# Modulation tiles beside the key and value projections, and query tiles woven into attention, in a two-layer model kernel

## The chip, the cores and the metric

The kernel runs on one core of a Trainium2 chip. The metric is the device time of one execution in microseconds (us), median over runs. The engines are TensorE (PE, with its weight loads PEld), VectorE (DVE), ScalarE (ACT), GpSimd (POOL) and SyncE (SP), which issues the weight loads. PE writes to eight PSUM banks of 512 floats per partition.

## What is computed

The reference runs a hybrid layer (windowed attention and an RWKV-7 scan side by side, then a SwiGLU), and behind it two more blocks. The change touches only the front of the first layer, in fp32, for 256 tokens x and 256 context tokens xc with 2048 features:

```python
mod = silu(c) @ ada_w + ada_b              # 2048 x 12288: shifts, scales and gates; also for c_ctx
sh1, sc1, g1, sh2, sc2, g2 = split(mod, 6)
z  = modulate(rmsnorm(x,  norm1_g), sh1,  sc1)  @ w_in
zc = modulate(rmsnorm(xc, norm1_g), sh1c, sc1c) @ w_in
# columns of w_in: q (16 heads of 64), k and v (4 heads), then for RWKV r, k, v, decay, a, gate
q, k = axial_rope(q), axial_rope(k)
attn = windowed_gqa(q, k, v, kc, vc, sink)   # 32 blocks of 128 queries, softmax over 512 keys
kk = k_r * k_k;  kk = kk * rsqrt(max(sum(kk * kk), 1e-12))   # per RWKV head
```

Of mod, the first third (sh1, sc1) is needed before z. The rest, "late modulation", is needed only after RWKV.

## The kernel before

Each weight matrix is cut into tiles of 512 rows by 256 columns, 512 KB each. `weight_stream` writes out by hand the one order in which all tiles come (`TILES`). SP issues their loads in that order into a ring of six buffers `raw` (NRAW = 6): the load of tile j waits until tile j - 6 has been used. The loop order on every engine is that of the generators in `schedule`, which has to take tiles in just the order of the stream; `run_all` weaves generators by numbers of steps for each.

An fp32 product is made of fp32r halves. ACT copies a tile to its high half `wh` (L1326), and the low half `wl = raw - wh` is made by DVE for tiles of even number (L1766) and by POOL for odd ones (L2298). `split_ahead` issues these splits when a tile is taken, for the stream's next AHEAD = 3 tiles; four pairs of halves exist. A `gemm` tile is then 24 matmuls (L872): of 512 columns where x and the context go together ("both": w_k, w_v, w_wa, w_ka), of 256 where only x does (w_q, w_r, w_gd). w_va has 48 of 256.

A modulation tile ("ada", L832) isn't split: PE multiplies it straight from `raw` in four row groups of 32 columns. After four tiles ACT copies the partial sums (`part`), PE adds the groups with a small matmul (`ada_sum`, L841), and DVE adds the bias.

The stages before: 64 early modulation tiles woven with 64 memory tiles; normalization of context and x into `halves`; w_k (4 outputs of 4 tiles each), w_v (the same), w_wa, w_ka, w_va; then the 16 w_q tiles, each followed by one of 16 late modulation tiles; then attention with r and the gate (16 w_r tiles, 4 w_gd), two of these tiles for each half step of attention, and behind them the 112 late modulation tiles left, woven with `keys`; then a fence and RWKV.

`attn` is a generator of 65 steps: first scores of blocks 0 and 1 (L901); then for every block n one step with the transposes of its probabilities (L915) and the scores of block n + 2, and one step with its product with the values (L926). ACT and DVE do the softmax between. `ev_q` ends a w_q output: ACT copies the raw values (`tm`), PE rotates them (L880), POOL and DVE finish.

`keys` is a generator of 17 steps: eight squares on ACT with sums over each head on PE (L940), one step for maximum, root and reciprocal, and eight steps in which ACT widens the scales (`sq`), PE transposes them (L948) and DVE multiplies to `kk`.

Of the kernel before, what the change touches and what calls it, by code (L numbers as in the profile page):

```python
# [165 lines left out]
class Program:  # L166
# [67 lines left out]
    def names(self):  # L234
# [28 lines left out]
        self.parts = [al[:, 3072 + 256 * i:3328 + 256 * i] for i in range(2)]  # L263
# [30 lines left out]
    def schedule(self):  # L294
# [12 lines left out]
        for n in range(4):  # L307
            rest(self.gemm("w_k", n, range(4), both, "v2", lambda j, n=n: self.ev_shift2(j, self.kT, 2 * n, 8 + 2 * n)))
        for n in range(4):
            rest(self.gemm("w_v", n, range(4), both, "v2", lambda j, n=n: self.ev_shift2(j, self.vT, 2 * n, 16 + 2 * n)))  # L310
        rest(self.gemm("w_wa", 0, range(4), both, "v2", lambda j: self.ev_shift2(j, self.wdad, 0, 24)))
        rest(self.gemm("w_ka", 0, range(4), both, "s2", self.ev_kA))
        token_major = [(a, 256 * tb, "A", 0, ("HA", "HB")[a], tb) for a in range(2) for tb in range(2)]
        rest(self.gemm("w_va", 0, range(4), token_major, "s2", self.ev_vA))
# [99 lines left out]

    def ada_tile(self, t):
        pass
# [41 lines left out]
    def queries(self):  # L458
        self.ada_active = True
        for n in range(4):  # L460
            yield from self.gemm("w_q", n, range(4), self.xonly, "s", lambda j, n=n: self.ev_q(j, n))
        self.ada_active = False
# [165 lines left out]
    def keys(self):  # L628
        yield from range(17)
# [164 lines left out]
class Tensor(Program):  # L794
# [28 lines left out]
    def ada_tile(self, t):  # L823
        raw = self.raw_of(t).rearrange("p (c n) -> p c n", c=4)
        b = 2 + t.nt % 2
        if t.kg == 0:
            self.bank(b, "mod_v", t.nt)
        self.wait_ge("silu_v", "sc16")
        self.wait_ge(f"raw{t.j % NRAW}", t.j)
        for g in range(4):  # L830
            k = 4 * t.kg + g
            m = self.e.matmul(self.G(b)[32 * g:32 * g + 32, 0:256], self.sc16[:, 32 * k:32 * k + 32], raw[:, g, :],  # L832
                              start=(t.kg == 0), stop=(t.kg == 3), skip_group_check=True)
        m.then_inc(self.sig("ada_mm", t.a), 1)
        self.last_a = t.a

    def ada_sum(self, nt):
        self.wait_ge("part_s", nt)
        part = self.part(nt)
        for fb in range(2):  # L840
            m = self.e.matmul(self.G(2 + nt % 2)[:, 256 + 2 * fb:258 + 2 * fb], part[:, 128 * fb:128 * fb + 128], self.cst("sel", 2),  # L841
                              start=True, stop=True, skip_group_check=True)
        m.then_inc(self.sig("ada_end", nt), 1)
# [32 lines left out]
    def rope_product(self, R, raw, rot):  # L876
        x = 2 + R % 2 if R < 10 else 3
        self.bank(4 + x, "rope_v", (R, "sin"))
        self.wait_ge(*raw)
        self.e.matmul(self.X(x)[:, 0:256], rot, self.tm[R % 4], start=True, stop=True).then_inc(self.sig("rope_mm", R), 1)  # L880
# [52 lines left out]
    def keys(self):  # L933
        squares = self.A("sq")
        self.bank(0, "kk_v", "max")
        o = self.G(0)[:, 0:64].rearrange("p (b c h) -> p b c h", b=4, c=8)
        for c in range(8):
            self.wait_ge("kk_s", ("sq", c))
            for b in range(4):
                m = self.e.matmul(o[:, b, c, :], squares[:, c, 128 * b:128 * b + 128], self.blk[:, ::64], start=True, stop=True)  # L940
            m.then_inc(self.sig("kk_mm", c), 1)
            yield
        yield
        for c in range(8):
# [375 lines left out]
class Scalar(Program):  # L1320
# [46 lines left out]
    def ada_part(self, nt):  # L1367
# [5 lines left out]
        if nt >= 16:  # L1373
            self.wait_fence(self.hb_free)
        self.wait_ge("ada_mm", self.last_a)
        self.act(self.part(nt), self.G(2 + nt % 2)[:, 0:256], ACT.Copy).then_inc(self.sig("part_s", nt), 1)
# [60 lines left out]
    def ev_gd(self, job):  # L1437
        self.wait_ge("mm", job.n)
        for fb in range(2):
# [59 lines left out]
    def keys(self):  # L1499
        self.wait_ge("mm", self.used["HA"])  # L1500
        for c in range(8):
            self.act(self.A("sq")[:, c, :], self.kT[:, c, :], ACT.Square, scale=self.cst("k_k", 8)[:, c:c + 1]).then_inc(self.sig("kk_s", ("sq", c)), 1)
# [5 lines left out]
        yield  # L1508
        for c in range(8):
# [250 lines left out]
class Vector(Program):  # L1760
# [80 lines left out]
    def ada_sum(self, nt):  # L1841
        dst = self.mod[:, 4 * nt:4 * nt + 4].rearrange("p (f t) -> p f t", t=2)
        src = self.G(2 + nt % 2)[:, 256:260].rearrange("p (f t) -> p f t", t=2)
# [33 lines left out]
    def rope_rest(self, R, dst, sin):  # L1877
        x = 2 + R % 2 if R < 10 else 3
# [3 lines left out]
        self.tt(raw, self.X(x)[:, 0:256], sin, MUL).then_inc(self.sig("rope_v", (R, "sin")), 1)  # L1882
# [78 lines left out]
    def keys(self):  # L1961
# [4 lines left out]
        self.ts1(inverse, self.G(0)[:, 0:64], 1e-12, None, MAX).then_inc(self.sig("kk_v", "max"), 1)  # L1966
        self.wait_ge("kk_s", "rt")
        self.e.reciprocal(inverse, inverse).then_inc(self.sig("kk_v", "rc"), 1)
        yield
        for c in range(8):  # L1970
# [443 lines left out]
def memory(nc, base):  # L2414

    m = {}
# [54 lines left out]
    at("inv", 24 * K, [4, 8, 2])  # L2471
# [132 lines left out]
```

## Time and profile before

| what | us |
|---|---|
| median of 3 runs | 4450.2 (4447.34 to 4452.76) |
| the profiled execution's own time | 4439.16 |
| its span | 4437.4 |
| PE busy | 4060.0 (91%) |
| DVE, ACT, POOL busy | 1525.7, 1580.5, 1355.4 |
| mean DMA rate | 151 GB/s |

Busy time of PE says that an instruction was in flight, not that PE was at its peak. The granted clock is a share of 2.4 GHz: 1.00 is the upper of TensorE's two levels and 0.50 the lower, and a window's value is the mean over it. "idle before" in square brackets is the time that an engine stood idle before an instruction, with what released it. All times are counted from the start of the span.

### The profile page before, as it was taken

How to read it: one execution, taken by the hardware profiler on the slowest of the kernel's cores; microseconds unless marked ns; L12 is line 12 of the kernel's file. 1: busy time of each engine (PE TensorE's matmuls, PEld its weight loads, DVE VectorE, ACT ScalarE, POOL GpSimd, SP SyncE). 2: the span in 40 equal slices, each digit the busy share in tenths (PEclk: the TensorE clock that was granted, in tenths of full speed). 3: DMA queues.
4: the chain of work that ended last, by engine and by line, in shares of the span. 5: the costliest groups of instructions: out<-in, count | busy, mean ns of one | idle time of the engine just before them, and what ended most of it. 6: DMA issues, size and time to landing. Idle time of an engine off the chain costs nothing.

```text
span 4437.4 us, 95544 instructions
## 1 busy us (share of the span) xinstructions
PE 4060.0 (91%) x42564; PEld 3794.0 (86%) x42564; DVE 1525.7 (34%) x2074; ACT 1580.5 (36%) x1986; POOL 1355.4 (31%) x632
## 2 busy tenths in 40 slices
PE   6979999979988889999997999897999999999978
PEld 5867887558887889999997899797899999999978
DVE  2133233446664543233334233325222222222232
ACT  3332233421223344343343343334333333333333
POOL 2322231000001334444442343443333333333333
PEclk8989998979998999999998999998999999999989
DMA  5862253830001445555553444353544444444433
GB/s 211 300 243 90 96 195 103 326 149 4 4 5 69 153 143 185 183 183 183 185 176 121 139 168 149 127 175 128 169 165 162 153 151 149 160 159 160 146 126 134
DMA packets 181879, 668.39 MB, mean 151 GB/s; under 512 B 20288, under 2 KB 20288, under 8 KB 180704
## 3 DMA queue, kind: packets, MB, share of 16 engines
q1 hardware_dynamic: 175248, 642.07, 42.3%
q10 hardware_dynamic: 4944, 16.03, 1.0%
q8 instruction: 337, 5.52, 0.5%
q0 software_dynamic: 1280, 4.20, 0.2%
q14 instruction: 70, 0.57, 0.0%
HBM read 653.82 MB, written 8.39 MB: 149 GB/s over the span
## 4 chain that ended last, share of the span: by engine, by line
PE 84%; DVE 6%; ACT 4%; issue 3%; DMA 1%; POOL 1%; ACTq 0%; POOLq 0%; DVEq 0%; SPq 0%
PE ps L872 65%; PE ps L832 2%; PE ps L1075 2%; PE ps L1099 2%; PE ps L1089 1%; PE ps L1011 1%; ACT wh L1326 1%; DVE wl L1766 1%; ACT halves L1326 1%; PE ps L1314 1%; PE ps L901 1%; DVE tm L1769 1%; PE ps L814 1%; PE ps L1298 1%; PE ps L926 1%
## 5 line engine op out<-in xcount | busy, mean ns | idle before, releaser
L872 PE MATMUL ps<-halves,wh 128*128 128x256 f32 (+1 forms) x13632 | 2620.4, 293 | 118.1 <-DVE halves L1769 34.0
L872 PEld LDWEIGHTS ps<-halves,wh 128*128 128x128 f32 x13632 | 2188.6, 195 | 178.6 <-issue 86.1
L872 PE MATMUL ps<-halves,wl 128*128 128x256 f32 (+1 forms) x6816 | 1983.4, 291 | 0.0
L2298 POOL TENSOR_TENSOR wl<-raw,wh 128x1024 fp32r<-128x1024 f32 x508 | 1237.1, 2436 | 1994.5 <-ACT wh L1326 1994.3
L1326 ACT ACTIVATE wh<-raw 128x1024 fp32r<-128x1024 f32 x1016 | 1072.9, 1058 | 1511.6 <-PE ps L872 1302.9
L1766 DVE TENSOR_TENSOR wl<-raw,wh 128x1024 fp32r<-128x1024 f32 x508 | 694.5, 1368 | 2062.9 <-ACT wh L1326 2062.8
L872 PEld LDWEIGHTS ps<-halves,wl 128*128 128x128 f32 x6816 | 1328.5, 195 | 12.8
L872 PE MATMUL ps<-wh,halves 128*128 128x256 f32 x2688 | 497.5, 285 | 0.0
L872 PEld LDWEIGHTS ps<-wh,halves 128*128 128x128 f32 x2688 | 423.3, 192 | 10.2 <-issue 7.8
L872 PE MATMUL ps<-wl,halves 128*128 128x256 f32 x1344 | 380.6, 283 | 0.0
L2298 POOL TENSOR_TENSOR halves<-mix,halves 128x1024 fp32r<-128x1024 f32 (+1 forms) x16 | 30.2, 1900 | 773.3 <-ACT halves L1326 773.3
L872 PEld LDWEIGHTS ps<-wl,halves 128*128 128x128 f32 x1344 | 258.3, 192 | 0.3
L1326 ACT ACTIVATE work<-ps 128x512 f32<-128x512 f32 x170 | 100.2, 592 | 226.5 <-PE ps L872 167.8
L832 PE MATMUL ps<-raw,sc 128*32 128x256 f32 x1536 | 126.7, 414 | 5.8 <-DMA raw<-in_ada 5.3
L1075 PE MATMUL ps<-X,BT 64*64 64x64 f32 x2560 | 95.9, 222 | 6.7 <-issue 6.0
L1075 PEld LDWEIGHTS ps<-X,BT 64*64 64x64 f32 x2560 | 87.3, 138 | 11.0 <-issue 9.2
L1306 PE MATMUL ps<-const,xw 128*128 128x128 f32 x144 | 24.1, 299 | 78.7 <-DVE xw L1772 78.7
L1099 PE MATMUL ps<-Xt,T 64*64 64x32 f32 x2560 | 93.2, 221 | 2.9 <-issue 2.6
L1326 ACT ACTIVATE hbl<-ps 128x256 f32<-128x256 f32 (+1 forms) x96 | 43.7, 455 | 133.9 <-PE ps L915 60.3
L1099 PEld LDWEIGHTS ps<-Xt,T 64*64 64x64 f32 x2560 | 86.6, 137 | 4.2 <-issue 3.3
L1306 PEld LDWEIGHTS ps<-const,xw 128*128 128x128 f32 x144 | 16.6, 150 | 85.0 <-DVE xw L1772 85.0
L832 PEld LDWEIGHTS ps<-raw,sc 128*32 128x32 f32 x1536 | 33.3, 111 | 56.9 <-issue 32.6
(241 smaller groups left out, 2669.8 us busy)
## 6 DMA issues: line engine op xcount, KB each, us to landing
raw<-in_ffn SPq DMA_DIRECT2D x264, 512.0 KB, 3.9
raw<-in_ada SPq DMA_DIRECT2D x192, 512.0 KB, 5.2
raw<-in_w_kv SPq DMA_DIRECT2D x192, 512.0 KB, 3.4
raw<-in_w_in_b SPq DMA_DIRECT2D x160, 512.0 KB, 3.8
raw<-in_w_in_a SPq DMA_DIRECT2D x128, 512.0 KB, 3.5
raw<-in_mem SPq DMA_DIRECT2D x64, 512.0 KB, 5.6
raw<-in_w_out_a SPq DMA_DIRECT2D x48, 512.0 KB, 4.0
raw<-in_w_out_b SPq DMA_DIRECT2D x48, 512.0 KB, 4.0
```

Source lines behind the costliest of these rows:

```text
L814: m = self.e.matmul(self.X(x)[:, 0:T], self.ones, self.work4[q][:, c, :], start=(q == 0 and c == 0), stop=(q == 3 and c == 3))
L832: m = self.e.matmul(self.G(b)[32 * g:32 * g + 32, 0:256], self.sc16[:, 32 * k:32 * k + 32], raw[:, g, :], start=(t.kg == 0), stop=(t.kg == ...
L872: p = self.e.matmul(o, x, y, start=bi not in begun, stop=final and kc == 3 and m == 2, skip_group_check=True)
L901: self.e.matmul(self.X(n % 2), self.qT[r, c, 128 * qb:128 * qb + 128], self.kA[r, c // 4, :], start=True, stop=True).then_inc(self.sig("at ...
L926: m = self.e.matmul(self.X(3)[HALF[half], 128 * qb:128 * qb + 128], self.vA[:, k, 64 * kv:64 * kv + 64], pt[:, k, :], start=(k == 0), stop ...
L1011: m = self.e.matmul(o[h, s, c, :], lhs(r, s, d, c), rhs(r, s, d, c), start=True, stop=True)
L1075: m = self.e.matmul(o[h, c, :], q["BT"][h, s, c, :], q["X"][h, s, c, :], start=True, stop=True)
L1089: m = self.e.matmul(o[h, c, :], q["Xt"][h, s, c, :], self.even(T1[h, s, c, :], lv), start=True, stop=True)
L1099: m = self.e.matmul(o[h, c, :], T1[h, s, c, :], self.odd(q["Xt"][h, s, c, :], lv), start=True, stop=True)
L1326: return self.e.activation(out, in_, func, **kw)
L1766: return self.e.tensor_tensor(out, a, b, op)
L2298: return self.e.tensor_tensor(out, a, b, op)
```

## The change

The stream and the weaving get another order:

- Behind each of the 32 w_k and w_v tiles come three late modulation tiles (96), behind each of the 12 tiles of w_wa, w_ka and w_va two (24), and behind each of the first four w_q tiles two (8). That is all 128.
- The 12 other w_q tiles are woven with attention's first 24 steps, one tile to two steps; then the 20 tiles of r and the gate with the rest, again one to two, and with one step of `key_norms` each.
- `keys` is cut into `key_norms` (9 steps) and `key_scales` (8 steps). The scales run alone, after attention.
- Late modulation uses PSUM banks 4 and 5 in place of 2 and 3; its partial sums, the squares and `inv` lie elsewhere. The squares have two buffers, so the square of c waits for the sum of c - 2.

```diff
-    for name, n in (("w_k", 4), ("w_v", 4), ("w_wa", 1), ("w_ka", 1), ("w_va", 1)):
-        add(name, range(n))
-    late = [("ada", nt, kg) for nt in range(16, 48) for kg in range(4)]
-    for i, q in enumerate([("w_q", nt, kg) for nt in range(4) for kg in range(4)]):
-        names += [q, late[i]]
+    late = iter([("ada", nt, kg) for nt in range(16, 48) for kg in range(4)])
+    for name, n, beside in (("w_k", 4, 3), ("w_v", 4, 3), ("w_wa", 1, 2), ("w_ka", 1, 2), ("w_va", 1, 2), ("w_q", 1, 2)):
+        for w in [(name, nt, kg) for nt in range(n) for kg in range(4)]:
+            names += [w, *itertools.islice(late, beside)]
+    add("w_q", range(1, 4))
     add("w_r", range(4))
     add("w_gd", range(1))
-    names += late[16:]
...
+        late_ada = self.ada_rest()
+        key_value = [self.gemm("w_k", n, range(4), both, "v2", lambda j, n=n: self.ev_shift2(j, self.kT, 2 * n, 8 + 2 * n)) for n in range(4)]
+        key_value += [self.gemm("w_v", n, range(4), both, "v2", lambda j, n=n: self.ev_shift2(j, self.vT, 2 * n, 16 + 2 * n)) for n in range(4)]
+        run_all((chain(*key_value), 1), (limited(late_ada, 96), 3))
...
+        run_all((chain(*narrow), 1), (limited(late_ada, 24), 2))
         self.hb_free = self.fence()
-        self.late_ada = self.ada_rest()
-        run_all((self.queries(), 1), (limited(self.late_ada, 16), 1))
-        run_all((self.attn(), 1), (chain(self.r_and_gd(), alternate(self.late_ada, self.keys())), 2))
+        run_all((self.queries(range(1)), 1), (late_ada, 2))
         self.ada_end()
+        attention = self.attn()
+        run_all((self.queries(range(1, 4)), 1), (limited(attention, 24), 2))
+        run_all((self.r_and_gd(), 1), (attention, 2), (self.key_norms(), 1))
+        rest(self.key_scales())
...
+    def ada_bank(self, nt):
+        return (2 if nt < 16 else 4) + nt % 2
...
+    def key_norms(self):
+        self.wait_fence(self.hb_free)
         for c in range(8):
-            self.act(self.A("sq")[:, c, :], self.kT[:, c, :], ACT.Square, scale=self.cst("k_k", 8)[:, c:c + 1]).then_inc(self.sig("kk_s", ("sq", c)), 1)
+            if c >= 2:
+                self.wait_ge("kk_mm", c - 2)
+            self.act(self.A("sq2")[:, c % 2, :], self.kT[:, c, :], ACT.Square, scale=self.cst("k_k", 8)[:, c:c + 1]).then_inc(self.sig("kk_s", ("sq", c)), 1)
             yield
```

In the changed kernel L844 is the modulation matmul, L853 its sum, L884 the tile's matmuls, L913, L927 and L938 the scores, transposes and values of attention, L952 the key norms, L963 the key scales, and L1341 every operation of ACT.

The order of ACT where the normalization of context and x (`halves`) ends, before:

```order
 L1326 ACTIVATE wh<-raw 128x1024 x5
 L1326 ACTIVATE tm<-ps 128x256
 L1326 ACTIVATE work<-ps 128x512
 L1326 ACTIVATE halves<-tm,mod 128x256 x32
 L1326 ACTIVATE wh<-raw 128x1024 x4
 L1326 ACTIVATE xk<-ps,tsr 128x512 x2
```

and after the change:

```order
 L1341 ACTIVATE halves<-tm,mod 128x256 x32
 L1341 ACTIVATE wh<-raw 128x1024 x2
 L1341 ACTIVATE work<-ps 128x256
 L1341 ACTIVATE wh<-raw 128x1024
 L1341 ACTIVATE work<-ps 128x256
 L1341 ACTIVATE wh<-raw 128x1024
 L1341 ACTIVATE xk<-ps,tsr 128x512 x2
```

Before, three splits of w_k stand in front of the normalization and the fourth behind it; now one stands in front, since two of the next three tiles of the stream are modulation tiles. Copies of partial sums (`work<-ps`) stand between the splits.

The order of PE in the w_k stage after the change, between two tiles of w_k:

```order
L884 MATMUL ps<-halves,wl 128x512
L844 MATMUL ps<-raw,sc_109 32x256 x12
L853 MATMUL ps<-const,work 128x2 x2
L884 MATMUL ps<-halves,wh 128x512 x2
```

Three modulation tiles (twelve matmuls) and a sum have moved in there; before, the L872 rows of two tiles follow each other.

The order of PE at two key norms before:

```order
L832 MATMUL ps<-raw,sc_108 32x256 x4
L940 MATMUL ps<-const,sq 128x2 x4
L915 MATMUL ps<-const,hbl_71 128x128 x4
L901 MATMUL ps<-work,hb_q 128x512
L832 MATMUL ps<-raw,sc_108 32x256 x4
L940 MATMUL ps<-const,sq 128x2 x4
L926 MATMUL ps<-hbl_71,work 64x128 x4
```

and at one of them after, with the end of one w_r tile and the start of the next:

```order
L884 MATMUL ps<-halves,wl 128x256
L938 MATMUL ps<-hbl_71,work 64x128 x4
L927 MATMUL ps<-const,hbl_71 128x128 x4
L913 MATMUL ps<-work,hb_q 128x512
L952 MATMUL ps<-const,sq_105 128x2 x4
L884 MATMUL ps<-halves,wh 128x256 x2
```

The norm now follows the scores with nothing between, and a whole w_r tile stands between it and the next block's values.

## Rows read from the trace of the kernel before

**Rows 1.** The page's head

```profile
span 4437.4 us, 95544 instructions
```

**Rows 2.** Windows: length, busy us (instructions) of PE, PEld, DVE, ACT, POOL, clock, DMA share, GB/s

```profile
645.00:720.00 75.00, 75.00 (x562) 67.22 (x566) 36.97 (x69) 32.66 (x60) 22.92 (x12) 1.00 0.43 141
720.00:780.00 60.00, 51.69 (x264) 33.16 (x262) 15.07 (x44) 21.38 (x47) 0.00 (x0) 0.63 0.30 97
780.00:895.00 115.00, 110.81 (x1028) 61.27 (x1026) 47.36 (x148) 50.01 (x133) 0.00 (x0) 1.00 0.89 336
895.00:928.00 33.00, 26.20 (x231) 11.12 (x224) 1.14 (x7) 3.60 (x9) 0.00 (x0) 0.73 0.87 345
928.00:980.00 52.00, 38.47 (x833) 33.86 (x834) 29.07 (x41) 17.05 (x20) 0.00 (x0) 0.64 0.11 39
```

**Rows 3.** Timeline of PE (start, us, instruction, idle before) at the restart

```profile
353.68 1.19 PE L872 MATMUL ps<-halves,wh 128*128 128x512 f32 x2 [5.99 <-ACT wh L1326]
```

**Rows 4.** Evictions of w_k and w_v (min/median/max ns, first to last start); start of w_q

```profile
L1326 ACT ACTIVATE xk<-ps,tsr x8: 679/685/691, 361.2 to 427.1; 128x512 f32<-128x512 f32 x8
...
L1326 ACT ACTIVATE vT<-ps,tsr x8: 681/686/692, 448.3 to 514.2; 128x512 f32<-128x512 f32 x8
...
582.76 0.51 PE L872 MATMUL ps<-halves,wh 128*128 128x256 f32 x2 [0.69 <-ACT work L1326]
```

**Rows 5.** Timeline of the query stage; then DMA issues of 820 to 880 us

```profile
604.89 0.64 PE L832 MATMUL ps<-raw,sc 128*32 128x256 f32 x8
605.46 0.61 PE L841 MATMUL ps<-const,hbl 128*128 128x2 f32 x4
605.92 0.48 PE L872 MATMUL ps<-halves,wh 128*128 128x256 f32 x2
606.01 0.38 SPq L2393 DMA_DIRECT2D raw<-in_w_q  x1
610.74 1.06 ACT L1326 ACTIVATE wh<-raw 128x1024 fp32r<-128x1024 f32 x1 [2.87 <-DMA raw<-in_w_q]
611.95 2.37 POOL L2298 TENSOR_TENSOR wl<-raw,wh 128x1024 fp32r<-128x1024 f32 x1 [6.08 <-ACT wh L1326]
...
raw<-in_ada SPq DMA_DIRECT2D x45, 512.0 KB, 5.7
```

**Rows 6.** Timeline of one block of attention with a key norm

```profile
747.33 0.63 PE L915 MATMUL ps<-const,hbl 128*128 128x128 f32 x4
748.94 0.64 PE L832 MATMUL ps<-raw,sc 128*32 128x256 f32 x8
750.22 0.71 ACT L1326 ACTIVATE sq<-xk,const 128x512 f32<-128x512 f32 x1
750.99 1.05 PE L940 MATMUL ps<-const,sq 128*128 128x2 f32 x8 [0.87 <-ACT sq L1326]
751.16 0.49 DVE L1772 TENSOR_SCALAR hbl<-hbl,cols 128x512 f32<-128x512 f32 x1
751.97 1.09 PE L926 MATMUL ps<-hbl,work 128*64 128x128 f32 x8
752.99 0.67 PE L832 MATMUL ps<-raw,sc 128*32 128x256 f32 x8
```

**Rows 7.** Timeline: last rope, first scores, first scaling; the last modulation sum

```profile
644.98 1.10 PE L880 MATMUL ps<-tm,const 128*128 128x256 f32 x4
...
646.01 1.98 PE L901 MATMUL ps<-work,hb_q 64*128 64x512 f32 x4
...
651.81 0.49 DVE L1772 TENSOR_SCALAR hbl<-hbl,cols 128x512 f32<-128x512 f32 x1
...
926.57 1.01 PE L841 MATMUL ps<-const,hbl 128*128 128x2 f32 x4 [0.56 <-ACT hbl L1326]
```

**Rows 8.** Timeline: a low half of POOL and the scaling of probabilities on DVE

```profile
700.73 1.57 POOL L2298 TENSOR_TENSOR wl<-raw,wh 128x640 fp32r<-128x640 f32 x1 [6.17 <-ACT wh L1326]
700.79 1.79 DVE L1772 TENSOR_SCALAR hbl<-hbl,cols 128x512 f32<-128x512 f32 x1
```

More of the change, by code:

```diff
@@ L262, in names @@
         self.ptbuf = [al[:, 1536 + 512 * i:2048 + 512 * i].rearrange("p (b n) -> p b n", b=4) for i in range(3)]
-        self.parts = [al[:, 3072 + 256 * i:3328 + 256 * i] for i in range(2)]
+        self.parts = [wk[:, 7168 + 256 * i:7424 + 256 * i] for i in range(2)]
         self.sink = self.cst("sink", 16)
@@ L306, in schedule @@
         xonly = self.xonly
[L307 to L312, printed above, removed]
+        late_ada = self.ada_rest()
+        key_value = [self.gemm("w_k", n, range(4), both, "v2", lambda j, n=n: self.ev_shift2(j, self.kT, 2 * n, 8 + 2 * n)) for n in range(4)]
+        key_value += [self.gemm("w_v", n, range(4), both, "v2", lambda j, n=n: self.ev_shift2(j, self.vT, 2 * n, 16 + 2 * n)) for n in range(4)]
+        run_all((chain(*key_value), 1), (limited(late_ada, 96), 3))
         token_major = [(a, 256 * tb, "A", 0, ("HA", "HB")[a], tb) for a in range(2) for tb in range(2)]
-        rest(self.gemm("w_va", 0, range(4), token_major, "s2", self.ev_vA))
+        narrow = [self.gemm("w_wa", 0, range(4), both, "v2", lambda j: self.ev_shift2(j, self.wdad, 0, 24)),
+                  self.gemm("w_ka", 0, range(4), both, "s2", self.ev_kA),
+                  self.gemm("w_va", 0, range(4), token_major, "s2", self.ev_vA)]
+        run_all((chain(*narrow), 1), (limited(late_ada, 24), 2))
         self.hb_free = self.fence()
-        self.late_ada = self.ada_rest()
-        run_all((self.queries(), 1), (limited(self.late_ada, 16), 1))
-        run_all((self.attn(), 1), (chain(self.r_and_gd(), alternate(self.late_ada, self.keys())), 2))
+        run_all((self.queries(range(1)), 1), (late_ada, 2))
         self.ada_end()
+        attention = self.attn()
+        run_all((self.queries(range(1, 4)), 1), (limited(attention, 24), 2))
+        run_all((self.r_and_gd(), 1), (attention, 2), (self.key_norms(), 1))
+        rest(self.key_scales())
         self.rwkv()
@@ L456, in memory_kv, with queries @@
         self.ada_active = False
-    def queries(self):
+    def queries(self, ns):
         self.ada_active = True
-        for n in range(4):
+        for n in ns:
             yield from self.gemm("w_q", n, range(4), self.xonly, "s", lambda j, n=n: self.ev_q(j, n))
@@ L626, with key_scales @@
     bonus_begin = bonus_a = bonus_k = bonus_v = nothing
-    def keys(self):
-        yield from range(17)
+    def key_norms(self):
+        yield from range(9)
+    def key_scales(self):
+        yield from range(8)
     def out_mean(self, p):
@@ L876, in rope_product @@
     def rope_product(self, R, raw, rot):
-        x = 2 + R % 2 if R < 10 else 3
-        self.bank(4 + x, "rope_v", (R, "sin"))
+        b = self.rope_bank(R)
+        self.bank(b, "rope_v", (R, "sin"))
         self.wait_ge(*raw)
-        self.e.matmul(self.X(x)[:, 0:256], rot, self.tm[R % 4], start=True, stop=True).then_inc(self.sig("rope_mm", R), 1)
+        self.e.matmul(self.G(b)[:, 0:256], rot, self.tm[R % 4], start=True, stop=True).then_inc(self.sig("rope_mm", R), 1)
     def ev_kA(self, job):
@@ L929, in attn, with key_norms @@
             yield
[L933 to L936, printed above, removed]
+    def key_norms(self):
+        squares = self.A("sq2")
+        self.bank(2, "kk_v", "max")
+        o = self.G(2)[:, 0:64].rearrange("p (b c h) -> p b c h", b=4, c=8)
         for c in range(8):
@@ L939, in keys @@
             for b in range(4):
-                m = self.e.matmul(o[:, b, c, :], squares[:, c, 128 * b:128 * b + 128], self.blk[:, ::64], start=True, stop=True)
+                m = self.e.matmul(o[:, b, c, :], squares[:, c % 2, 128 * b:128 * b + 128], self.blk[:, ::64], start=True, stop=True)
             m.then_inc(self.sig("kk_mm", c), 1)
@@ L943, in keys, with key_scales @@
         yield
+    def key_scales(self):
+        squares = self.A("sq")
         for c in range(8):
@@ L1508, in keys, with key_scales @@
         yield
+    def key_scales(self):
+        inverse = self.A("inv")
+        self.wait_ge("mm", self.used["HA"])
         for c in range(8):
@@ L1881, in rope_rest @@
         self.wait_ge("rope_g", R)
-        self.tt(raw, self.X(x)[:, 0:256], sin, MUL).then_inc(self.sig("rope_v", (R, "sin")), 1)
+        self.tt(raw, self.G(self.rope_bank(R))[:, 0:256], sin, MUL).then_inc(self.sig("rope_v", (R, "sin")), 1)
         self.wait_ge("rope_v", (R, "sin"))
```

26 lines of the change are left out of this document (14 added, 12 removed).

## The prediction

> **What bounds the kernel now.** I read the table of windows first, because the change touches one stretch only. After the restart at 353.68 the sequence is: w_k and w_v tiles to about 513.5, the three narrow projections to 582.76, the queries to 646, r and the gate woven with the first heads to about 720, then heads with late modulation and key norms, then modulation tiles alone to 927.6, then RWKV. In the windows [rows 2] 645 to 720 is TensorE (PE) without a gap at granted clock 1.00. 720 to 780 has 51.7 us of work in 60 and clock 0.63, so most of it ran at the lower of the two levels (1.2 instead of 2.4 GHz). 895 to 928 has 26.2 in 33, clock 0.73, with the DMA share at 0.87: tiles that wait for their loads. So the stretch loses time in two ways: the slow clock beside thin work, and a transfer-bound tail. From 582.76 to 927.6 it takes 344.8 us. The same matmuls back to back at full clock would take about 300 (priced below). **About 45 us are to be had there, and that is the ceiling of any gain.** The view of order and the timeline rows say what the new order loses in their place.
>
> **Prices at full clock.** A "both" tile (w_k, w_v): evictions of xk go from 361.2 to 427.1 over 12 tiles, less the 0.6 between two evictions of a pair, 65.3 / 12 = 5.44 us; vT gives the same (65.9 - 0.6) / 12 [rows 4]. A modulation tile: 604.89 to 605.46, 0.57 us, and per four tiles one sum of 0.46 (605.46 to 605.92) [rows 5]: 0.685 each. An x-only tile: the query stage of 16 tiles lasts from 582.76 [rows 4] to 646.0 (behind the rope of 644.98, 1.10 us [rows 7]); less 16 modulation tiles (11.0) and four rope pairs (4.4) it is 47.8 / 16 = 3.0. One head-block of attention: transposes and next scores 747.33 to 748.94 = 1.61, values 751.97 to 752.99 = 1.02, together 2.63; one key norm 750.99 to 751.97 = 0.98 [rows 6]. Sum for 36 x-only tiles (108), 128 modulation tiles (88), 32 head-blocks (84), 8 norms and 8 scales at about 1.0 (16) and rope (4.4): 300.
>
> **The change, walked forward from the restart.**
>
> *Restart.* Before, three w_k tiles were split ahead of the normalization and multiplied during it; PE then waited 5.99 us for the fourth, whose split stands behind the normalization on ScalarE (ACT) [rows 3]. The planner splits three tiles of the stream ahead, and now these are one w_k tile and two modulation tiles, of which nothing is split. So at 353.68 only one w_k tile and three modulation tiles are done: two tiles lost, 10.9, less three modulation tiles, 2.1: **8.8 us**. The same PE start otherwise.
>
> *Key and value tiles.* Tile 1 ends at about 361.2, where tile 3 ended. 30 more at 5.44 + 3 x 0.685 = 7.49 are 224.7, and three last modulation tiles 2.1: 588.0. Transfers: 45 tiles in the 60 us from 820 to 880 are 1.33 us each [rows 5], so a group of four needs 5.3 of 7.5 us; bandwidth hides it. Latency nearly doesn't. The raw ring has six places, and a w tile's load is issued when the second modulation tile two groups ahead is done: E + 1.2, with E the end of the w tile before last. A w_q load as second of a pair is issued at 606.01 and split from 610.74 on, 4.7 later [rows 5]; the split takes 1.06, the low half on GpSimd 2.37 from 611.95 (on VectorE, every other tile, about half of it). Ready at E + 1.2 + 4.7 + 1.2 + 2.4 = E + 9.5; PE comes at E + 2.05 + 5.44 + 2.05 = E + 9.5. Every other tile is on the edge: I take 0.3 us for 15 of them, **4 us** (bounds 0 and, with the 5.7 us of the full queue, 15 x 1.3 = 20). 592.
>
> *Narrow projections.* Before 513.5 to 582.8, 69.3; 24 modulation tiles add 16.3: 677.6. Their groups are longer per load, nothing waits.
>
> *First query tile and the end of modulation.* 4 x 3.0 + 8 x 0.685 + rope 1.1 and 1.5 of waits at the two ends: 697.7. Transfers 12 x 1.33 = 16 are covered.
>
> *Heads, queries, r, gate.* 32 tiles x 3.0 = 96, 32 head-blocks x 2.63 = 84: 877.7 without waits. Each round is: tile, values of block n, transposes and scores. Scores end at 748.94, the probabilities of the next block are done at 751.65 (751.16 + 0.49) [rows 6]: 2.7 us, while PE has 3.0 + 1.0 of other work. Rounds without extras therefore lose nothing. Four places do:
> - Start: the second query tile covers nothing for the first transposes, since both first scores and the transposes stand behind it in one piece. Before, the softmax of block 0 took from the scores' start at 646.01 to the end of the scaling at 652.30 (651.81 + 0.49), 6.3, of which the scores are 2.0 [rows 7]; two r tiles covered the rest, now nothing does. The rope that delayed VectorE there comes a tile earlier, so I take **3.9 us** of the 4.3.
> - Rope of three query tiles: ACT's copies stand behind the exponent and the sink of that round, which is where the square starts, 750.22, 1.3 after the scores' end [rows 6]; with the copy itself the rotation waits about 1.75, and PE has nothing between: 3 x (1.1 + 1.75) = **8.6**, of which 3.3 is work.
> - Key norms: the order shows L952 right behind the scores. Its square on ACT comes behind the exponent too: from the scores' end at 748.94 to the norm's start at 750.99 are 2.05 [rows 6]; before, a modulation tile filled 1.1 of it and 0.87 was idle, now nothing fills it. 8 x (2.05 + 0.98) = **24.2**, and 1.5, an estimate, for ACT's table changes around the root.
> - Scales at the end: they stand alone. ACT first does the gate's copies, two tanh and a mix copy: PE idle 3.9, then 8 x 1.0 and 0.8 for the last product: **13**.
> 877.7 + 3.9 + 8.6 + 25.7 + 13 = 928.9.
>
> *The clock.* It was 1.00 where dense tiles ran without waits (645 to 720), 0.63 where heads, norms and waits of 0.9 to 2.7 us alternated [rows 2]. A key round now is 3.0 of dense work in 8.7. Bounds: no loss, or all eight rounds at half, 8 x 6.6 = 53. I take the end near the dense rows, 1.2 us a round, 10 in all, 2 at the start of attention and 3 in the scales: **15 us**.
>
> Sum: 943.9 where before has 927.6 (926.57 + 1.01 [rows 7]), **+16 us**. RWKV and what follows have the same order and the same fence, 0. The execution traced has a span of 4437.4 [rows 1] and a time of 4439.2: 4455. The median of the runs shown, 4450.2, is 11 above it, so 4466.
>
> **The rivals.** A measurement of this kernel tells apart about 0.2%, 9 us.
> 1. *The forecast*, +6 to +30: chance 0.42.
> 2. *Dense tiles hold the clock.* Every key round holds a full x-only tile; if that is enough, 15 us go and the stretch ends at 928.9, +1: no change. For it: clock 1.00 in 780 to 895, where no dense tile ran at all, though PE there was busy for 110.8 of 115 us [rows 2]. Against: PE idle 2.05 in each key round. 0.20.
> 3. *The other side: RWKV opens at full clock.* Before, PE entered it from a slow tail, and 928 to 980 has clock 0.64 on 38.5 us of work [rows 2]; 0.72 of these at half cost up to 14. If the clock holds in the key rounds too and PE enters with it, the end is +1 - 14 = -13, 4437. It decides from the point where less than 5 us of the clock loss is paid. Against: the wait for RWKV's own tables after the fence stays. 0.20.
> 4. *Loads set the pace beside w_k and w_v.* If the second load of a burst of four takes the 5.7 us of the full queue [rows 5] and not 4.7, GpSimd's tiles come 1.0 to 1.3 late each: 16 to 20 in place of 4, +30, 4480. 0.11.
> 5. *VectorE waits for GpSimd beside the heads.* The scaling of the probabilities took 1.79 us instead of 0.49 when GpSimd's low half started 0.06 ahead of it [rows 8]. All heads now run beside splits. With a low half of 2.37 starting first the probabilities would come 2.6 later, 1.2 after PE needs them, on the 16 rounds where GpSimd splits: 19 more, +35, 4485. Against: its split follows ACT's, which stands behind the exponent, so the scaling is usually first by 0.3. 0.07.
> The Trainium skill, "SBUF — State Buffer", section "Who interferes with whom", says why this could be: VectorE in a two-port mode and GpSimd lock one pair of ports for a whole instruction, and issue order decides who blocks. By that rule the price is paid in full whenever GpSimd is first, and the trace agrees (1.79 against 0.49); taken alone, without the 0.3 us of lead, it would give rival 5.
>
> **How the numbers follow.** The range 4436 to 4490 holds rivals 1, 2 and most of 3, 4 and 5. For the forecast alone it is 4456 to 4480. Slower by over 0.2%: 0.38 of the forecast and rivals 4 and 5, 0.56. Within: rival 2 and the rest of the forecast, 0.24. Faster: rival 3, 0.20.
>
> **What would show it.** PE's restart with tile 1 at 353.7 and the end of w_v near 592; PE idle at L952 about 2 us eight times; first rope of attention behind an idle of 1.8; the scales ending near 944; windows of the key rounds with clock 0.75 to 0.95. Wrong if low halves come late beside w_k by over 1 us each, if the key rounds show clock 1.00, or if RWKV's first 50 us differ in clock from before.

## The result, and the profile after

| | us | executions |
|---|---|---|
| before | 4449.43 | 4 (4447.34 to 4452.76) |
| after | 4481.92 | 4 (4473.66 to 4486.98) |

The ratio is 1.0071, interval 1.0053 to 1.0088: **0.7% slower, 32 us**. The profiled execution took 4481.41. Before's profiled one took 4439.16, 10 under its median, so the two traces lie 42 apart and not 32. The first 32 of them are in the stretch that the change touches: RWKV's first product starts at 936.40 before and 968.93 after.

The page's head, against [rows 1]:

```profile
span 4479.6 us, 95520 instructions
```

The restart on PE's timeline, which answers to [rows 3], and the last eviction of w_v on ACT's, which answers to [rows 4]:

```profile
353.27 1.19 PE L884 MATMUL ps<-halves,wh 128*128 128x512 f32 x2 [16.06 <-issue]
...
598.43 1.26 ACT L1341 ACTIVATE vT<-ps,tsr 128x512 f32<-128x512 f32 x2 [2.10 <-PE ps L884]
```

This is w_k's tile 1, as forecast: TensorE has stood for 16.06 us where before it stood for 5.99. With three modulation tiles behind it, w_v ends at 600.5 (598.43 and 2.1). What PE waited for from 353 to 600 (us in total, times, longest):

```profile
PE ps L884 <- issue: 16.4, 2, 16.1
PE ps L884 <- POOL wl L2319: 9.5, 13, 1.5
```

Thirteen times it was the low half that GpSimd makes of every other tile. From the first query tile to attention (PE's timeline, against [rows 5, 7]):

```profile
700.84 0.77 PE L884 MATMUL ps<-halves,wh 128*128 128x256 f32 x2 [1.70 <-POOL wl L2319]
...
707.52 0.48 PE L884 MATMUL ps<-halves,wh 128*128 128x256 f32 x2
...
710.55 1.12 PE L913 MATMUL ps<-work,hb_q 64*128 64x512 f32 x2
712.28 1.12 PE L913 MATMUL ps<-work,hb_q 64*128 64x512 f32 x2 [0.60 <-DVE mod L1786]
717.10 1.11 PE L927 MATMUL ps<-const,hbl 128*128 128x128 f32 x4 [3.70 <-DVE hbl L1792]
...
740.84 1.57 PE L892 MATMUL ps<-tm,const 128*128 128x256 f32 x4 [1.63 <-ACT tm L1341]
```

Modulation ends at 707.5; one query tile later come the first scores, and then 3.70 us of idle for the first probabilities. The first rope product inside attention waits 1.63. One round with a key norm, PE and ACT together, against [rows 6]:

```profile
844.85 0.71 ACT L1341 ACTIVATE sq<-xk,const 128x512 f32<-128x512 f32 x1
...
845.62 1.05 PE L952 MATMUL ps<-const,sq 128*128 128x2 f32 x8 [1.97 <-ACT sq L1341]
845.79 0.49 DVE L1792 TENSOR_SCALAR hbl<-hbl,cols 128x512 f32<-128x512 f32 x1
...
851.08 1.09 PE L938 MATMUL ps<-hbl,work 128*64 128x128 f32 x8
852.10 0.66 PE L927 MATMUL ps<-const,hbl 128*128 128x128 f32 x4
852.68 1.12 PE L913 MATMUL ps<-work,hb_q 64*128 64x512 f32 x2
...
855.77 1.05 PE L952 MATMUL ps<-const,sq 128*128 128x2 f32 x8 [1.97 <-ACT sq L1341]
```

From norm to norm it is 10.15 us (855.77 - 845.62). Work at the upper clock is 3.0 + 2.63 + 0.98 = 6.6 of it, 1.97 is idle for the square, and the rest, near 1.5, is lost because part of the tile behind runs at the lower clock. The end of the stretch:

```profile
945.56 1.09 PE L938 MATMUL ps<-hbl,work 128*64 128x128 f32 x8 [0.69 <-ACT hbl L1341]
949.56 9.65 PE L963 MATMUL ps<-const,sq 128*128 128x128 f32 x64 [2.91 <-ACT sq L1341]
968.93 1.97 PE L1001 MATMUL ps<-wup,lora 64*64 64x512 f32 x4 [9.72 <-DMA w0r<-in_w]
```

The windows, against [rows 2]:

```profile
353.00:600.00 247.00, 236.82 (x1576) 170.06 (x1580) 43.35 (x68) 50.75 (x69) 35.59 (x16) 0.99 0.73 258
600.00:710.00 110.00, 107.78 (x813) 86.47 (x805) 22.87 (x32) 26.65 (x38) 26.04 (x14) 0.98 0.69 244
710.00:800.00 90.00, 80.72 (x469) 62.87 (x468) 48.83 (x101) 39.21 (x86) 21.02 (x13) 0.89 0.28 89
800.00:880.00 80.00, 64.16 (x364) 53.78 (x364) 24.92 (x60) 29.60 (x62) 9.27 (x4) 0.84 0.17 50
880.00:944.00 64.00, 64.00 (x432) 51.27 (x431) 30.61 (x77) 31.99 (x72) 8.01 (x5) 0.99 0.06 17
944.00:970.00 26.00, 12.68 (x83) 10.90 (x83) 8.80 (x21) 9.08 (x18) 0.00 (x0) 0.80 0.21 74
```

The transfer-bound tail is gone, as the change meant. In its place 800 to 880 has 16 us without work and clock 0.84; 880 to 944, rounds of a tile and a head-block without a norm, has no idle time and clock 0.99. So the woven rounds as such are sound, and the norm is the first suspect for what spoils the others.

### The profile page after: what moved, and what is told of

It reads as the page before. It is cut to its first block, busy times and chain, and to the rows that moved or that the text cites. A ratio compares the mean times of both kernels' runs of the same rounds, so it can differ in the third digit from the quotient of the medians.

```text
span 4479.6 us, 95520 instructions
## 1 busy us (share of the span) xinstructions
PE 4071.7 (91%) x42564; PEld 3813.7 (85%) x42564; DVE 1533.6 (34%) x2074; ACT 1574.5 (35%) x1986; POOL 1349.9 (30%) x632
## 4 chain that ended last, share of the span: by engine, by line
PE 82%; DVE 6%; ACT 5%; issue 3%; DMA 2%; POOL 1%; ACTq 0%; POOLq 0%; DVEq 0%; SPq 0%
PE ps L884 63%; PE ps L1090 2%; PE ps L844 2%; PE ps L1114 2%; ACT wh L1341 2%; PE ps L1026 1%; PE ps L1104 1%; DVE wl L1786 1%; ACT halves L1341 1%; POOL wl L2319 1%; DMA raw<-in_w_v 1%; PE ps L826 1%; PE ps L1329 1%; DVE tm L1789 1%; PE ps L913 1%
## 5 line engine op out<-in xcount | busy, mean ns | idle before, releaser
L884 PE MATMUL ps<-halves,wh 128*128 128x256 f32 (+1 forms) x13632 | 2647.4, 295 | 137.1 <-DVE halves L1789 33.7
L884 PEld LDWEIGHTS ps<-halves,wh 128*128 128x128 f32 x13632 | 2204.0, 197 | 214.0 <-issue 131.2
L884 PE MATMUL ps<-halves,wl 128*128 128x256 f32 (+1 forms) x6816 | 1993.9, 293 | 0.0
L1341 ACT ACTIVATE wh<-raw 128x1024 fp32r<-128x1024 f32 x1016 | 1070.0, 1055 | 1543.7 <-PE ps L884 1176.7
L884 PEld LDWEIGHTS ps<-halves,wl 128*128 128x128 f32 x6816 | 1339.0, 196 | 13.6
L884 PE MATMUL ps<-wh,halves 128*128 128x256 f32 x2688 | 498.6, 285 | 0.1
L884 PEld LDWEIGHTS ps<-wh,halves 128*128 128x128 f32 x2688 | 423.9, 192 | 10.6 <-issue 9.2
L884 PE MATMUL ps<-wl,halves 128*128 128x256 f32 x1344 | 380.9, 283 | 0.0
L884 PEld LDWEIGHTS ps<-wl,halves 128*128 128x128 f32 x1344 | 258.5, 192 | 0.2
L1341 ACT ACTIVATE work<-ps 128x512 f32<-128x512 f32 (+1 forms) x202 | 112.3, 558 | 278.1 <-PE ps L884 169.0
L844 PE MATMUL ps<-raw,sc 128*32 128x256 f32 x1536 | 109.2, 387 | 0.0
L1090 PEld LDWEIGHTS ps<-X,BT 64*64 64x64 f32 x2560 | 88.6, 140 | 12.3 <-issue 11.1
L1104 PE MATMUL ps<-T,Xt 64*64 64x32 f32 x2048 | 77.1, 223 | 5.3 <-issue 5.3
L1104 PEld LDWEIGHTS ps<-T,Xt 64*64 64x64 f32 x2048 | 72.7, 141 | 10.4 <-issue 9.3
```

Of the source, the lines that this page charges most:

```text
L884: p = self.e.matmul(o, x, y, start=bi not in begun, stop=final and kc == 3 and m == 2, skip_group_check=True)
L1090: m = self.e.matmul(o[h, c, :], q["BT"][h, s, c, :], q["X"][h, s, c, :], start=True, stop=True)
L1104: m = self.e.matmul(o[h, c, :], q["Xt"][h, s, c, :], self.even(T1[h, s, c, :], lv), start=True, stop=True)
L1341: return self.e.activation(out, in_, func, **kw)
```

## The experiments

Each is compared with executions of the kernel before that ran beside it; the changed kernel stands at 1.0071. "RWKV" is the start of RWKV's first product in the trace.

| run | ratio to before (interval) | against the changed kernel, us | RWKV, us | against 968.93 |
|---|---|---|---|---|
| norms_first | 1.0004 (0.9992 to 1.0017) | -30 | 938.90 | -30.0 |
| norm_filler | 1.0043 (1.0026 to 1.0060) | -12 | 954.84 | -14.1 |
| filler_half | 1.0072 (1.0047 to 1.0097) | 0 | 965.92 | -3.0 |
| lows_vector | 1.0041 (1.0029 to 1.0054) | -13 | 957.12 | -11.8 |
| restart3 | 1.0035 (1.0024 to 1.0047) | -16 | 958.25 | -10.7 |
| rope_late | 1.0040 (1.0027 to 1.0054) | -14 | 956.63 | -12.3 |
| part1_only | 1.0080 (1.0063 to 1.0098) | +4 | 976.42 | +7.5 |
| combo | 0.9944 (0.9926 to 0.9962) | -57 | 912.51 | -56.4 |
| combo_unwoven | 1.0014 (0.9998 to 1.0029) | -25 | 940.64 | -28.3 |
| combo_start | 0.9937 (0.9915 to 0.9959) | -60 | 904.30 | -64.6 |

The third column is the difference of the ratios times 4450; since each interval is 5 to 11 us to either side, and the changed kernel's own is 8, a few us in it mean nothing. The last column is read from single traces, and agrees with it within 5.3 us in each run.

**norms_first: the key norm ahead of the attention steps.**

```
-        run_all((self.r_and_gd(), 1), (attention, 2), (self.key_norms(), 1))
+        run_all((self.r_and_gd(), 1), (self.key_norms(), 1), (attention, 2))
```

> In the rounds of r and the gate the key norm stands ahead of the two attention steps (right behind the r tile), on every engine; nothing else differs from the changed kernel. Theory: the 1.97 to 2.06 us in which TensorE waits eight times for ScalarE's square are a matter of order alone, since the square then runs while the r tile is multiplied; and the stretch of 3.4 us at the lower clock in each of these rounds is caused by that wait. Both go: 8 x 1.97 = 16 and 8 x 1.7 = 14, together 26 to 30 us less than the changed kernel, and the windows of these rounds show clock 1.00. Rival A: the wait moves, since the first transposes of the round now stand behind only a tile and a norm while the square has pushed ScalarE's exponent back: 8 x 0.5 to 1.5 us of waits at the transposes, gain 5 to 15. Rival B: the clock does not follow the wait, gain 13 to 16.

PE's timeline of one round, norm to norm, and its window:

```profile
805.38 1.05 PE L952 MATMUL ps<-const,sq 128*128 128x2 f32 x8
806.37 1.09 PE L938 MATMUL ps<-hbl,work 128*64 128x128 f32 x8
807.39 0.66 PE L927 MATMUL ps<-const,hbl 128*128 128x128 f32 x4
...
812.02 1.05 PE L952 MATMUL ps<-const,sq 128*128 128x2 f32 x8
...
800.00:860.00 60.00, 59.43 (x411) 48.27 (x409) 28.07 (x69) 34.95 (x71) 9.61 (x4) 1.00 0.21 67
```

The round is 6.64 us instead of 10.15, there are no brackets (no idle time), and the clock is 1.00. One line's order was worth 30 us, almost the whole loss of the change: the theory at its upper end. Rival A's waits at the transposes are not there. How much of the 30 was idle time and how much the slow clock behind it is told by the next two.

**norm_filler and filler_half: the wait filled with work that nobody reads.**

```
+        hi = self.acts["HA"][0]
+        self.wait_ge("rope_v", (9, "sin"))
         for c in range(8):
+            for k in range(14):
+                self.e.matmul(self.G(3)[:, 0:256], hi[:, k, 0:128], hi[:, k, :], start=True, stop=True, skip_group_check=True)
             self.wait_ge("kk_s", ("sq", c))
```

In filler_half the 14 is a 7.

> The changed kernel with 14 more products of 128x128 by 128x256 on TensorE ahead of each wait for a square (their result is read by nobody); they are sized at 14 x 0.125 = 1.75 us, to fill the wait of 1.97 and end inside it. Theory: the lower clock in the key rounds comes from TensorE's idle time there; with it filled the windows of these rounds show clock near 1.00 and the kernel is 8 x 1.4 to 1.7 = 11 to 14 us shorter than the changed one, although it does more work. Rival: the clock falls for another reason (the thin work of attention itself); then it is the same or up to 8 x 1.5 = 12 us longer, as the added products take twice their time at the lower clock.

> As the run with added products, but 7 instead of 14: they take about 0.96 us of the 1.97 us wait, so TensorE still idles about 1.0 us in each of the eight key rounds. Theory (the lower clock follows an idle time of some size): either the remaining 1.0 us is short enough, then the round is 8.65 us as with 14 products and the kernel is as fast as that one (12 us under the changed kernel); or it is not, then the round stays near 10.15 and nothing is won. Both tell how large an idle time beside dense tiles costs here; I give 0.7 to the first, as idle times of 0.5 to 0.7 us stand in stretches of clock 1.00.

With 14 products, and then with 7 (PE's timeline and a window of each):

```profile
801.77 1.93 PE L953 MATMUL ps<-halves 128*128 128x256 f32 x14
803.81 1.05 PE L956 MATMUL ps<-const,sq 128*128 128x2 f32 x8
...
812.46 1.05 PE L956 MATMUL ps<-const,sq 128*128 128x2 f32 x8
...
800.00:860.00 60.00, 59.24 (x417) 49.26 (x416) 21.05 (x50) 25.48 (x53) 7.20 (x3) 1.00 0.19 59
```

```profile
813.04 1.05 PE L956 MATMUL ps<-const,sq 128*128 128x2 f32 x8 [0.95 <-ACT sq L1345]
...
821.14 1.09 PE L953 MATMUL ps<-halves 128*128 128x256 f32 x7
823.18 1.05 PE L956 MATMUL ps<-const,sq 128*128 128x2 f32 x8 [0.95 <-ACT sq L1345]
...
820.00:840.00 20.00, 18.11 (x106) 15.30 (x105) 7.15 (x17) 7.67 (x17) 2.38 (x1) 0.83 0.16 45
```

TensorE does more work and the kernel is 12 us shorter: the round is 8.65 us, which is 1.5 less than 10.15, eight times. That is the clock's own share, and the idle time's is the rest, 8.65 - 6.64 = 2.0 a round. With half the filler 0.95 us of idle remains before each of the eight norms. The first round was still clean (804.39 to 813.04, 8.65 us); from the second on the clock is 0.83, the round 10.14 (823.18 - 813.04), and in the median nothing is won. I had given 0.7 to the other outcome. An idle time of a microsecond in each such round cost the clock as much as one of two.

**lows_vector: low halves of w_k and w_v on VectorE.**

```
+def low_on_gpsimd(t):
+    return t.n % 2 and t.name not in ("w_k", "w_v")
...
-        self.wait_ge("lo_g" if t.n % 2 else "lo_v", t.n)
+        self.wait_ge("lo_g" if low_on_gpsimd(t) else "lo_v", t.n)
```

> The changed kernel with the low halves of all 32 w_k and w_v tiles on VectorE, in place of every other one on GpSimd. Theory: the 11.2 us in which TensorE waits 14 times for GpSimd's low half are the ring's latency plus GpSimd's 2.37 us for a low half; VectorE does it in about half, so these waits go: 9 to 11 us less than the changed kernel, and w_v's last eviction about 590 in place of 599. Rival: the load lands late by itself and the waits move to the high half or stay; gain below 3 us.

The waits of 353 to 600, and the last eviction of w_v:

```profile
PE ps L888 <- ACT wh L1345: 14.9, 1, 14.9
PE ps L888 <- DVE wl L1790: 0.9, 3, 0.4
...
587.31 1.27 ACT L1345 ACTIVATE vT<-ps,tsr 128x512 f32<-128x512 f32 x2 [1.10 <-PE ps L888]
```

587.31 instead of 598.43, and 9.5 us of waits became 0.9, so the rival is refuted. The gain, 13 us by the ratios and 11.8 in the trace, is slightly more than the theory's 9 to 11. In the changed kernel the loads of w_k and w_v landed 4.5 us after their issue in the median (400 to 590 us), as in the forecast; the time of GpSimd's low half was what came on top.

**restart3: three w_k tiles ahead of the first modulation tile.** The modulation tiles displaced stand three to a narrow tile.

```
-            names += [w, *itertools.islice(late, beside)]
+            names += [w, *itertools.islice(late, beside if name != "w_k" or w[1:] > (0, 1) else 0)]
...
+        rest(limited(key_value, 2))
-        run_all((chain(*key_value), 1), (limited(late_ada, 96), 3))
+        run_all((key_value, 1), (limited(late_ada, 90), 3))
```

> The changed kernel with the first three w_k tiles next to each other in the stream again, so that three are split ahead of the normalization; the modulation tiles taken from there stand beside the narrow projections (three to a tile in place of two). Theory: the two tiles lost at the restart (10.9 us, less three modulation tiles, 2.1) come back: 8 to 9 us less than the changed kernel, and a wait of up to 6 us behind the third tile as in the kernel before, of which three modulation tiles cover 2. Rival: loads beside the narrow projections now come too densely (three small tiles and one large in 7.5 us) and give part of it back: gain 3 to 6.

```profile
354.11 1.19 PE L886 MATMUL ps<-halves,wh 128*128 128x512 f32 x2 [4.86 <-issue]
```

The wait at the restart (PE's timeline) is 4.86 in place of 16.06, with three w_k tiles done by then and not one, and attention's first scores come at 701.49 in place of 710.55, 9.1 earlier: the theory's 8 to 9. RWKV's start is 10.7 earlier and the measured ratio gives 16; the expectation holds for the trace, and the 5 us between it and the median lie within the intervals.

**rope_late: the rope product of TensorE behind the next weight tile.** Tensor's `ev_q` only notes the two products, and `products` issues them behind its last matmul.

```
+        self.late_rope = [(self.ropes + fb, ("ev_s", (job.key, fb - 1))) for fb in range(2)]
...
         p.then_inc(self.sig("mm", t.n), 1)
+        self.ropes_now()
```

> The changed kernel with TensorE's rope products of the last three query tiles issued behind the next weight tile, in place of ahead of it. Theory: the three waits of 1.63 to 1.72 us for ScalarE's copies and the stretch of 3.4 us at the lower clock behind each come from that position alone: 3 x (1.67 + 1.7) = 10 us less than the changed kernel. Rival: the clock stays down here, because the first of these stretches stands close to the start of attention: gain 5.

```profile
739.11 1.03 PE L893 MATMUL ps<-tm,const 128*128 128x256 f32 x4
740.07 1.09 PE L947 MATMUL ps<-hbl,work 128*64 128x128 f32 x8
...
735.00:760.00 25.00, 25.00 (x161) 18.99 (x160) 14.22 (x30) 12.79 (x29) 6.38 (x4) 1.00 0.30 91
```

No wait, clock 1.00, where the changed kernel has 23.37 us of work in the same window at clock 0.93. From the first scores to the scales' first product it takes 229.2 us and not 239.0, so 9.8: the theory's 10.

**part1_only: the modulation tiles beside the projections, without weaving the query tiles.**

```
-        run_all((self.queries(range(1, 4)), 1), (limited(attention, 24), 2))
-        run_all((self.r_and_gd(), 1), (attention, 2), (self.key_norms(), 1))
+        rest(self.queries(range(1, 4)))
+        run_all((chain(self.r_and_gd(), self.key_norms()), 1), (attention, 2))
```

> Of the change, the modulation tiles beside the key and value projections alone: the last three query tiles stand by themselves ahead of attention, r and the gate and then the key norms are woven with it one to two, so 12 of the 32 head-blocks have no weight tile beside them. Theory: without a tile a round lacks 3.0 us of cover, waits 1 to 2.7 for the probabilities and runs at the lower clock: from the changed kernel, less the three waits and clock stretches of the ropes (10) and the eight at the key norms (up to 30), more 12 x (2 + 2.6) = 55: 15 to 30 us more than the changed kernel. Rival: heads by themselves are no slower than beside tiles, since ScalarE and VectorE are free of splits; then it is 10 to 30 us less than the changed kernel.

```profile
881.89 1.86 PE L952 MATMUL ps<-const,sq 128*128 128x2 f32 x8 [1.97 <-ACT sq L1341]
883.69 1.97 PE L938 MATMUL ps<-hbl,work 128*64 128x128 f32 x8
...
860.00:940.00 80.00, 58.88 (x237) 40.72 (x235) 23.34 (x68) 28.30 (x68) 0.00 (x0) 0.68 0.00 0
```

4 us more than the changed kernel, which the interval doesn't tell from none (7.5 in the trace): between the theory (15 to 30 more) and the rival (10 to 30 less), so neither came true. The bare heads are slow (21 us idle in 80, clock 0.68), and the norms, which I thought covered in this variant, still wait 1.97 each, now without a tile. The run shows that the second half of the change gained little or nothing as it was written. What weaving is worth by itself needs the variant below.

**combo: the four edits together** (norms_first, lows_vector, restart3, rope_late).

> Four edits together: key norm ahead of the attention steps, low halves of w_k and w_v on VectorE, the first three w_k tiles together at the restart, the last three rope products behind the next weight tile. Theory: the losses stand in different stretches and add up: 30 + 13 + 16 + 10 = 69 less than the changed kernel, near 4412, about 0.9% faster than the kernel before. Rival: two of them meet (VectorE's low halves with the restart's own, the key norms with the rope), and the sum falls short by 10 to 20: 4425 to 4435.

PE's timeline at attention's first scores and the scales' first product:

```profile
691.95 1.98 PE L928 MATMUL ps<-work,hb_q 64*128 64x512 f32 x4
...
892.43 10.35 PE L978 MATMUL ps<-const,sq 128*128 128x128 f32 x64 [2.92 <-ACT sq L1356]
```

4422, 0.56% faster than the kernel before, and 57 us less than the changed kernel where the theory had 69 and the rival 49 to 59. RWKV starts 56.4 us earlier than in the changed kernel; the four alone come to 64.8 (30.0 + 11.8 + 10.7 + 12.3). A part of the 8.4 between is no shortfall: norms_first and rope_late are 1.5 us earlier at attention's first scores too, where their code is the changed kernel's. By stretches the sum nearly holds: the scores are 18.6 us earlier (lows_vector alone 11.3, restart3 9.1), and from there to the scales it is 38.5 us less (norms_first alone 27.5, rope_late 9.8). So the losses are nearly independent. The 69 was 4 us above what the four traces sum to, mostly by restart3, put in with the 16 of its median where its trace has 10.7. Of the rival only the number fits: the one stretch that falls short, the first, does so by 1.8 us, no more than two traces of the same code differ there.

**combo_unwoven: the same with the last three query tiles ahead of attention.** The edit is the first line of part1_only's alone.

> The four edits together, but with the last three query tiles by themselves ahead of attention. Theory: once its own waits are gone, the weaving of the query tiles is worth what 12 more covered head-blocks save: modulation tiles beside the projections alone was 3 us over the changed kernel although it lacked the waits of the ropes (14) and of the key norms (30), so the weaving is worth 47: this is 40 to 50 us more than the four edits with it, 4462 to 4472, slower than before. Rival: uncovered heads cost less once the key norm is ahead of them: 20 us more, 4442.

```profile
884.27 1.12 PE L942 MATMUL ps<-const,hbl 128*128 128x128 f32 x4 [0.79 <-DVE hbl L1807]
...
850.00:915.00 65.00, 52.59 (x180) 30.31 (x178) 25.75 (x77) 23.44 (x64) 0.00 (x0) 0.61 0.00 1
```

RWKV starts 28.1 us later than in combo, 31 by the ratios. Weaving is worth about 30, between the theory's 40 to 50 and the rival's 20: an uncovered head waits only 0.79 once the first three are past (1.67 to 1.08), and most of its price is clock 0.61. My 47 was built on part1_only, where I had counted the norms as covered. The second half of the change is right in itself, and in the changed kernel its own waits ate nearly all of it.

**combo_start: four modulation tiles between the first scores and the first transposes.**

```
...
+        next(queries, None)
+        next(attention, None)
+        rest(self.ada(47))
+        next(attention, None)
+        self.ada_end()
...
```

The stream has these four tiles in the same place, and two modulation tiles instead of three beside each tile of w_va.

> The four edits, and the last four modulation tiles held back to stand between the first scores and the first transposes of attention (their sum behind the transposes). Theory: the 3.7 us in which TensorE waits for the first probabilities and the half clock behind it go, for 2.7 us of work that moves there and is not added: 4 to 6 us less than the four edits. Rival: the first scores, the mask and the exponent take 6.2 us and only 2.7 are covered, so an idle of 1 us and the slow clock stay: 3 us.

```profile
684.22 1.98 PE L941 MATMUL ps<-work,hb_q 64*128 64x512 f32 x4
686.13 1.93 PE L863 MATMUL ps<-raw,sc 128*32 128x256 f32 x32
689.90 0.66 PE L955 MATMUL ps<-const,hbl 128*128 128x128 f32 x4 [1.83 <-DVE hbl L1820]
```

The wait falls from 3.7 to 1.83, but the slow clock behind it does not go: 0.78 in 684.2 to 700, as against 0.79 in 692 to 708 of combo. RWKV starts 8.2 earlier than in combo, and only a small part of that arises where the theory put it. From the first scores to the scales it takes 201.5 us, 1.0 more than in combo, with four modulation tiles at the forecast's 0.685 each, 2.7 of work, added: 1.7 gained, less than even the rival's 3. Of the rest 2.1 arise ahead of w_v's last eviction, where the two hardly differ, about 3 between there and the scores, where combo waits 1.15 and 1.73 for halves of query tiles and this kernel does not, and 1.5 behind the scales' start. The measured 0.9937 against 0.9944 doesn't tell the two apart, so the gain stays open. By its median it is the fastest version: 4412.9, 0.63% under the kernel before.

## Why the prediction was right, and where its sizes were off

The forecast was slower by 16 us on the traced stretch (943.9 for 927.6), with a time of 4466 and a range of 4436 to 4490. Measured: slower, 4481.9, in the range but near its upper end, and 2 us outside the 4456 to 4480 that the forecast alone allowed; the rise was twice the size. The direction and the places of the losses were right. That rival 4's 4480 comes closest to the measured time is chance, as the key and value tiles below show. The stretch ended at 959.2 (949.56 + 9.65), 31.6 later than before. Waypoint by waypoint:

| step | forecast | measured | off by |
|---|---|---|---|
| restart, tile 1 | 353.7 | 353.27 | -0.4 |
| w_v with its modulation tiles done | 592 | 600.5 | +8.5 |
| modulation done | 697.7 | 707.5 | +9.8 |
| PE goes idle for the scales | 927.9 | 946.65 | +18.8 |
| scales done | 943.9 | 959.2 | +15.3 |
| RWKV's first product | 952.7 | 968.93 | +16.2 |

(927.9 is 928.9 less the 13 of the scales, with 12 of the 15 us of clock; 952.7 is 943.9 and the 8.8 that stood behind the modulation tail before.)

*Restart.* Right, and two tests bear it out: tile 1 after 16.06 us of idle, and 9.1 us back with three w_k tiles together.

*Key and value tiles: the ring's wait was mis-sized, the first of two such terms.* I took 4 us within bounds of 0 and 20; it was 9.5, thirteen waits of up to 1.5. I knew that ready time and need met to the tenth of a microsecond, and gave 0.3 us a tile to a sum of five estimated pieces; the middle of the bounds would have been nearer. Of the 8.5 us in the table these waits are 5.5; the other 3 are 0.4 at tile 1's end, a wait of 0.4 behind it, and 0.07 in each of 30 groups (361.64 to 369.20 is 7.56, where I had 7.49). lows_vector shows the cause: with the low half on VectorE 0.9 us remains, and w_v's last eviction comes at 587.3, with the modulation tiles behind it done near 589.4, so the no-wait pace (588.0) was right to 1.4. Rival 4 had another culprit, loads that land 5.7 us after their issue: they landed after 4.5 in the median, and its 16 to 20 us of waits were 9.5.

*Narrow projections, first query tile.* Right to 1.3 us, the one surprise being a wait of 1.70 for GpSimd's low half in the query tile, with a slow-clock tile behind it.

*Attention.* The idle times are as forecast: start 3.70 (3.9), ropes 1.63 to 1.72 (1.75), norms 1.97 to 2.06 (2.05), 24.5 us in all at the three places. *The clock was the second term mis-sized*, at two of its places: key rounds 1.2 us each where the fillers show 1.5, and the ropes 0 where the row of 740.84 (work of 1.0 us that took 1.57) and those behind it run at the lower clock, some 1.6 us each (rope_late: 9.8 us for waits of 5.0 in all). With 0.60 at the second scores and a long slow stretch behind the first ones (clock 0.66 in 710 to 725) this is most of the +9.0 between 707.5 and 946.65. The 1.5 us for ACT's table changes does not appear: PE has no idle time between the last norm and 944.

*Scales.* 12.6 us (2.91 idle, 9.65 of work); I had 13 and 3 of clock, so 3.4 too much.

*RWKV, 0.* What stands ahead of RWKV's first product explains the medians: 32.5 us there, 32 measured. From there to the last product that reads RWKV's state Z (L1175, start to start) the traces show 473.0 before and 480.4 after; over all runs here, in which that code is one and the same, it is 468.0 (restart3) to 481.3 (combo, one of the fastest), with no relation to the medians. So this spread belongs to the single executions, and why it falls so was not tested. The four edits, which take 56.4 us in the trace ahead of RWKV, take 57 in the measured time.

*Rivals.* 2 (dense tiles hold the clock) is refuted by the windows at 0.84, and norm_filler shows what does hold it. 3 (RWKV opens at full clock) did not come: 960.5 to 1012.5, the stretch that answers to 928 to 980 before, has clock 0.66 where that had 0.64, and the wait of 9.72 for its own tables stands ahead. 5 is refuted: the 32 scalings between 714 and 945 took 548 ns in the mean, 1.9 us in all over the 0.49 of a free one, where it wanted 19. Its price was also too high for its rows: in [rows 8] a low half of 1.57 made the scaling 1.3 longer, so one of 2.37 makes it about 2 longer and not 2.6.

## What to carry to other kernels

When filler work is moved away from a place, list what it covered there. The modulation tiles were more than a load-bound tail: one of them stood between scores and norm. TensorE paid twice for waiting a microsecond or two in each round for a small result, for the wait and for the slow clock behind it, and the cure was order alone: a dense tile between the issue of the producer and that of its consumer (one line, 30 us).

When ready time and need come out equal in an estimate with several pieces, take the middle of the bounds and not the near end, and look at the slowest engine in the chain: giving its work to a faster one took 13 us off here. A deeper ring was not tried.

If a change moves the time little or the wrong way, see first which of its rounds are clean. Here 880 to 944 was, without idle time and at clock 0.99, which said that the weaving was sound and that the rounds with extras needed mending. With those, the restart and the low halves mended, the kernel went from 0.7% slower to 0.6% faster.

## What the runs showed of the hardware that I had not expected

- An idle time of 0.95 us in each key round cost the same clock as one of 1.97 (windows at 0.83 and 0.84, rounds of 10.14 and 10.15), although 18.1 of 20 us were busy; only the first such round stayed at 1.00. With the gap filled it was 1.00 throughout.
- The length of a single gap does not decide it. Beside w_k, where rounds are dense tiles throughout, single waits of 1.49 us in the changed kernel and of 1.77 in filler_half (windows 433 to 443 and 432 to 442) left the clock at 1.00; one of 1.92 there (restart3) gave 0.83 over its 10 us. The windows of the first and the last:

```profile
433.00:443.00 10.00, 8.51 (x65) 5.81 (x58) 2.32 (x4) 2.75 (x5) 1.88 (x1) 1.00 0.66 220
```

```profile
465.58 0.70 PE L886 MATMUL ps<-halves,wh 128*128 128x512 f32 x2 [1.92 <-POOL wl L2321]
...
464.00:474.00 10.00, 8.42 (x40) 6.34 (x44) 1.23 (x1) 1.06 (x1) 1.44 (x1) 0.83 0.54 206
```

- More work made the kernel shorter: 112 products whose result nobody reads took 12 us off.
